# Hybrid SSD encoder with 16 experts: each expert's first weight chunk in transfers of 112, 8 and 8 partitions, and all finished rows normed ahead of the last sums

## The reference, cut to what matters

```python
def expert_choice_ffn(h, w_router, w_gate, w_up, w_down):
    ...
    cap = CAPACITY_FACTOR * n_tok // N_EXPERTS          # 64 and 32 tokens an expert
    probs = jax.nn.softmax(t.astype(jnp.float32) @ w_router.astype(jnp.float32), axis=-1)
    aff, idx = lax.top_k(probs.T, cap)
    xe = t[idx]
    hid = jax.nn.silu(jnp.einsum("ecd,edf->ecf", xe, w_gate)) * jnp.einsum("ecd,edf->ecf", xe, w_up)
    ye = jnp.einsum("ecf,efd->ecd", hid, w_down) * aff[..., None].astype(h.dtype)
    out = jnp.zeros_like(t).at[idx.reshape(-1)].add(ye.reshape(-1, d))
...
    x = x + expert_choice_ffn(rms_norm(x, norm_ffn_w), w_router, w_gate, w_up, w_down)
...
    return rms_norm(x, norm_final_w)
```

## Time and profile before

| | |
|---|---|
| median of 3 runs | 2410.2 us (2407.26 to 2411.43) |
| the profiled execution | 2407.7 us |
| its span | 2405.8 us |
| TensorE busy | 2370.5 us, 99% |
| VectorE, ScalarE, GpSimd busy | 1077.1, 519.3, 302.5 us |
| moved by DMA | 707.02 MB |
| chain that ended last | TensorE 47%, DMA 10% |

### The profile page before, as it was taken

One profiled execution on the slowest core, in us unless ns is written; L12 is line 12 of the kernel. 1 busy time (PEld: TensorE's weight loads), 2 busy tenths in 40 slices (PEclk: granted clock), 3 DMA queues, 4 the chain that ended last, 5 costly groups with the idle time before them and its releaser, 6 DMA issues.

```text
span 2405.8 us, 49544 instructions
## 1 busy us (share of the span) xinstructions
PE 2370.5 (99%) x21931; PEld 1625.6 (68%) x21931; DVE 1077.1 (45%) x2059; ACT 519.3 (22%) x1076; POOL 302.5 (13%) x417
## 2 busy tenths in 40 slices
PE   9999999999999999999999999999999999999997
PEld 8888999899898888745655455555555555444454
DVE  7989888888987634451221222122122112212213
ACT  6445444544534412200000000000000000000001
POOL 0422431341341000000000000000000000000001
PEclk9999999999999999999999999999999999999998
DMA  5233234223336545799999999999999999999996
GB/s 187 74 110 123 92 99 134 90 92 118 114 117 212 208 140 207 289 395 410 418 411 420 416 409 420 408 417 409 418 417 408 419 416 409 420 406 416 420 409 259
DMA packets 88646, 707.02 MB, mean 294 GB/s; under 512 B 11824, under 2 KB 16048, under 8 KB 51568
## 3 DMA queue, kind: packets, MB, share of 16 engines
q1 hardware_dynamic: 65504, 628.96, 64.4%
q0 software_dynamic: 14368, 56.80, 7.5%
q10 hardware_dynamic: 8560, 18.10, 2.0%
HBM read 669.76 MB, written 34.06 MB: 293 GB/s over the span
## 4 chain that ended last, share of the span: by engine, by line
PE 47%; DMA 10%; DVE 0%; issue 0%; POOL 0%; POOLq 0%; SPq 0%; ACT 0%; DVEq 0%
PE p_gu L2653 31%; PE p_y L2671 8%; DMA raw<-in_w_e 7%; PE p_y L2674 4%; PE p_z L2674 2%; DMA raw_first<-in_w_e 2%; DMA raw<-xa 1%; PE p_gu L1592 1%; DVE raw L2587 0%; DMA out<-raw 0%; DVE xg L2579 0%; POOLq L2725 0%; POOL out L2489 0%; PE off_banks L1606 0%; SPq L2421 0%
## 5 line engine op out<-in xcount | busy, mean ns | idle before, releaser
L2653 PE MATMUL p_gu<-raw,xT 128*32 128x512 f32 (+1 forms) x8160 | 888.6, 556 | 2.3 <-DMA raw<-in_w_e 2.2
L2653 PEld LDWEIGHTS p_gu<-raw,xT 128*32 128x32 f32 x8160 | 393.8, 110 | 362.8 <-issue 231.0
L2538 DVE SCALAR_TENSOR_TENSOR tg<-tg,p_gu 128x256 f32<-128x256 f32 (+1 forms) x144 | 57.4, 399 | 1051.6 <-ACT tg L2501 1047.1
L2671 PE MATMUL p_y<-raw,hidT 128*32 128x384 f32 x3744 | 433.3, 486 | 0.0
L1282 PE MATMUL pp<-h,wx_hi 128*128 128x256 f32 (+1 forms) x1664 | 423.9, 346 | 0.5 <-ACT fo L836 0.5
L2501 ACT ACTIVATE tg<-p_gu 128x256 f32<-128x256 f32 (+1 forms) x144 | 52.8, 367 | 1266.6 <-PE p_gu L2653 1249.0
L2674 PE MATMUL p_y<-raw,hidT 128*32 128x256 f32 x1248 | 319.5, 379 | 0.0
L1282 PEld LDWEIGHTS pp<-h,wx_hi 128*128 128x128 f32 x1664 | 282.9, 190 | 31.0 <-ACT fo L836 0.7
L1282 PE MATMUL pp<-h,wx_lo 128*128 128x256 f32 (+1 forms) x832 | 281.3, 338 | 0.0
L2674 PEld LDWEIGHTS p_y<-raw,hidT 128*32 128x32 f32 x1248 | 137.2, 110 | 100.1 <-issue 32.1
L2674 PE MATMUL p_z<-raw,hidT 128*32 128x256 f32 x624 | 184.8, 379 | 0.0
(11 more groups left out here) (297 smaller groups left out, 2951.1 us busy)
## 6 DMA issues: line engine op xcount, KB each, us to landing
raw<-in_w_e SPq DMA_DIRECT2D x185, 2048.0 KB, 32.0
raw<-in_w_e SPq DMA_DIRECT2D x58, 1536.0 KB, 32.5
raw_first<-in_w_e SPq DMA_DIRECT2D x23, 2048.0 KB, 33.3
w_raw<-in_w_x SPq DMA_DIRECT2D x48, 512.0 KB, 3.5
dec<-acs POOLq DMA_DIRECT2D x48, 512.0 KB, 4.8
raw<-in_w_e SPq DMA_DIRECT2D x16, 1024.0 KB, 32.6
w_raw<-in_w_g SPq DMA_DIRECT2D x24, 512.0 KB, 3.4
g_tab<-gx POOLq DMA_DIRECT2D x8, 1152.0 KB, 6.0
```

Source lines behind the costliest of these rows:

```text
L2538: dve.scalar_tensor_tensor(out=tg[:, r % 2, 0:w], in0=tg[:, r % 2, 0:w], scalar=1.0, in1=p[:, 0:w], op0=ALU.add, op1=ALU.mult).then_inc(s_ ...
L2653: mm = pe.matmul(p_gu[g][quad(q), 0:w], xT[:, e % 2, k * SLOTS + 32 * g:k * SLOTS + 32 * (g + 1)], slot[:, at:at + w], start=(k == 0), sto ...
L2671: pe.matmul(y_first[half][quad(g), :], hidden(g), w[:, half * 3 * P:(half + 1) * 3 * P], start=first, stop=last)
```

## The change

A chunk is loaded in pieces (`in_pieces`) if it is the first gate and up chunk of an expert and comes from the loop, which are 15 chunks. `load_part` then issues three transfers, of partitions 0 to 111, 112 to 119 and 120 to 127, each adding 16 to the slot's semaphore. `landings(c)` counts how much the semaphore of `c`'s slot has had with chunk `c`, and `loaded` waits for that. In the tail the roots are taken in groups of tiles 0 to 2, 3 and 4, and 5, and VectorE norms all six tiles ahead of `summed`. The squares stay behind the last tanh.

```diff
+PIECES = (slice(0, P - 16), slice(P - 16, P - 8), slice(P - 8, P))
+def in_pieces(c):
+    kind, b, i = chunk(c)
+    return c >= RAW and kind == "gu" and i == 0 and b % NB == 0
+def landings(c):
+    return sum(16 * (len(PIECES) if in_pieces(n) else 1) for n in range(c % RAW, c + 1, RAW))
...
-    sp.dma_start(raw[c % RAW][:, 0:w], src).then_inc(s_raw[c % RAW], 16)
+    for rows in PIECES if in_pieces(c) else (slice(0, P),):
+        sp.dma_start(raw[c % RAW][rows, 0:w], src[rows, :]).then_inc(s_raw[c % RAW], 16)
...
-        SQUARES_AT = ROUNDS - 1
-        NORMS_AT = ROUNDS - 1
-        ROOTS = (slice(0, 1), slice(1, 3), slice(3, NT))
-        FIRST_NORMS = 3
+        SQUARES_AT = {ROUNDS - 1: range(NT)}
+        ROOTS = (slice(0, NT // 2), slice(NT // 2, NT - 1), slice(NT - 1, NT))
...
-                if r == NORMS_AT:
-                    for t in range(FIRST_NORMS):
-                        norm(t)
+            for t in range(NT):
+                norm(t)
             summed(0)
             summed(1)
-            for t in range(FIRST_NORMS, NT):
-                norm(t)
...
-                pe.wait_ge(s_raw[c % RAW], (XT_LOADED if c % RAW < EARLY_RAW else 0) + 16 * (c // RAW + 1))
+                pe.wait_ge(s_raw[c % RAW], (XT_LOADED if c % RAW < EARLY_RAW else 0) + landings(c))
```

More of the change, by code:

```diff
@@ L2522, in _ @@
                         result(e)
-                if r == SQUARES_AT:
-                    for t in range(NT):
-                        square(t)
+                for t in SQUARES_AT.get(r, ()):
+                    square(t)
             act.wait_ge(f_row, 1)
```

## The result

The changed kernel takes 2634.16 us (median of 6 runs, 2630.86 to 2644.86), the kernel before 2408.55 (6 runs): 1.094 times the time, 95% interval 1.0919 to 1.096. The forecast was 2403.5 in a range up to 2422. 225 us were lost where 5 were expected to be gained.

What follows compares the result with a forecast made beforehand. Weight loads on the slowest DMA engines were taken to bound the last experts. Stall -4.79, squares -3.2 and new tail +2.7 gave -5.3 us; with half the median's excess given back, 2403.5 us, range 2399.5 to 2422.

Steps and rivals of the forecast that it cites:

- What bounds the kernel: In the last experts TensorE waits for weight chunks, 4.79 us in all, because the slowest DMA engines need 86.5 us an expert.
- The stall by growth and head start: TensorE's stall is lag growth, 1.34 us an expert, times 11.6 experts, less a prefetch head start of 10.7 us: 4.79 us.
- I take 0.63, since a row stays one packet of one engine: In the weight transfers, a 16 KB row of a narrow piece takes 0.63 us of its engine, as in whole loads.
- Rival 3: Narrow weight transfers are slow: 1.5 us an expert more on the nine-row engines, 2422 us in all; chance 0.13.
- Its bound from above: Row time in narrow weight transfers taken from the gather, 325 GB/s instead of 414: 1.27 times, applied to 9 rows.
- The estimate by the Trainium skill: 8 partitions reach two ports, so 128 KB takes 2.4 us instead of 0.63; a stall of 37 us, near 2446.
- Rival 1: The extra weight rows fall on the engines that lag: growth 1.97 us an expert, 10.1 us lost, 2420; chance 0.15.
- Were the eight the ones that do not lag: In the weight stream, the slowest engines would then lag 0.71 us an expert instead of 1.34: no stall, -4.79 us.
- That the instruction packets lie on the engines that lag: Eight engines lag together and carry all instruction packets seen; these cost 0.5 us an expert over sixteen engines, 1.0 over eight.
- The squares: In the tail, rows of xa land 4.6 us sooner against TensorE's end, so the squares follow the last tanh: -3.2 us.
- The new tail: Sums behind all six norms make the put wait for the last scaling: +2.7 us, or +1.8 with a short last root.
- The other roots end before VectorE wants them: In the tail, VectorE's norms never wait for roots after the first group; six norms run at 1.23 us each.

Runs made afterwards that it cites:

- the share alone: New tail, whole loads, plus four small transfers of 8 rows four partitions apart (0 to 31) behind each piece chunk, into unread columns: 2420.92 us, 8.8 over the new tail without them.
- one event at expert 2: New tail, pieces of 112, 8 and 8 partitions in expert 2 only, all other chunks whole: 2420.46 us; the same in expert 9 only: 2425.19 us.

## Why the prediction was wrong, point by point

**What bounds the kernel** held: TensorE waits for nothing but weights, and the slowest engines set the pace. The stall by growth and head start fits the run of the share alone, if the slowest engines are among its eight: a row more on these was to cost 7.4 us, and 8.8 were measured.

**The step that failed** is the price of the pieces: "I take 0.63, since a row stays one packet of one engine." A row does stay one packet, but its time depends on the other rows in flight with it. Measured, a row took some 1.15 us while the 112 rows passed and up to 2.3 while the 8-row pieces did, and on all sixteen engines. Three things were missed. The 112 rows were costed at nothing; an extra transfer of 112 partitions an expert costs 55 us by itself. The slow rate holds for the loads that run beside the pieces, not for nine rows of eight engines. And it holds from the first engine's arrival to the last one's departure, so engines that are out of step multiply it: 8.4 us for one event at expert 2, 13.1 at expert 9, and 222 / 15 = 14.8 each when every expert has one.

**Rival 3** named the mechanism and the side, and was off in size: 1.5 us an expert and 2422 against 14.8 and 2634. Its bound from above, 1.27 times a row's time from the gather, was no bound: the nearest row of the trace was of another kind of transfer, and it was applied to the wrong rows. The estimate by the Trainium skill, "SBUF — State Buffer", section "Door 1: The DMA port swizzle", 2446, had the better price for a piece of 8 rows (2.4 us, where rows took up to 2.3) and the same fault, that only eight engines pay.

**Number of engines.** That a short transfer takes eight engines was taken from a page alone. The packets now show it: 65744 - 65504 = 240 = 15 x 16, two times 8 completions for each chunk more, as the Trainium skill, "DMA: Bandwidth & Descriptors", section "Why a DMA increments its semaphore by 16 and not by 1", has it. That these are the lowest-numbered engines stands in that section too, and no row shows it.

**Rival 1** (the wrong eight) was priced at 7.4 us for the share and seems to be true in part, with two lagging engines among the eight. By the run of the share alone, the change would then have lost some 8.8 us even with free pieces, and not gained 4.8. So this step of the forecast, "Were the eight the ones that do not lag", most likely failed as well. In the changed kernel it is hidden: even shares cost as much. That the instruction packets lie on the engines that lag, as the prediction reads them, can't be told from the record, in which no packet names its engine; what the landings show is two groups of eight.

**Issues and completions** were costed at nothing, and cost nearly nothing: 2.6 us for thirty more transfers and 256-column rows.

**The squares** were to follow the last tanh at once (-3.2 us). They wait as before, 3.02 us. The engines ended later and not earlier, and TensorE with them; with whole loads the wait is 3.00.

**The new tail** was right in sum, and partly by luck. ScalarE, GpSimd and VectorE in the tail of the changed kernel:

```profile
2600.50 0.33 ACT L2514 ACTIVATE tg<-p_gu 128x192 f32<-128x192 f32 x1 [0.96 <-PE p_gu L2662]
2603.85 1.06 ACT L2529 ACTIVATE raw<-raw 128x1024 f32<-128x1024 f32 x1 [3.02 <-DMA raw<-xa]
```

```profile
2610.18 1.16 POOL L2489 TENSOR_SCALAR ssqf<-ssqf 128x2 f32<-128x2 f32 x1 [1.41 <-ACT raw L2529]
2611.42 1.62 POOL L2490 TENSOR_TENSOR rstdf<-ssqf,neg_half 128x2 f32<-128x2 f32 x1
...
2614.49 1.47 POOL L2490 TENSOR_TENSOR rstdf<-ssqf,neg_half 128x1 f32<-128x1 f32 x1
...
2621.22 0.55 POOL L2496 TENSOR_TENSOR rstdf<-ssqf,neg_half 96x1 f32<-96x1 f32 x1
2624.18 1.05 POOL L2502 DMA_INDIRECT out<-xg,idx_g  x1 [2.41 <-issue]
```

```profile
2608.80 3.68 DVE L2599 SCALAR_TENSOR_TENSOR raw<-raw,rstdf,nfin 128x1024 f32<-128x1024 f32 x3 [6.78 <-POOL rstdf L2490]
2613.07 2.48 DVE L2599 SCALAR_TENSOR_TENSOR raw<-raw,rstdf,nfin 128x1024 f32<-128x1024 f32 x2 [0.59 <-POOL rstdf L2490]
2615.99 1.28 DVE L2599 SCALAR_TENSOR_TENSOR raw<-raw,rstdf,nfin 128x1024 f32<-128x1024 f32 x1 [0.44 <-POOL rstdf L2490]
2617.19 0.61 DVE L2587 SCALAR_TENSOR_TENSOR xg<-p_y,aff,xg 96x384 f32<-96x384 f32 x1
...
2621.81 1.41 DVE L2637 SCALAR_TENSOR_TENSOR xg<-xg,rstdf,nfin 96x512 f32<-96x512 f32 x2 [1.86 <-POOL rstdf L2496]
```

From the first square to the put it takes 2624.18 - 2603.85 = 20.3 us, before 17.5: +2.8, where 2.7 was predicted. Two misses cancel. "The other roots end before VectorE wants them" was wrong: beside VectorE's norms the roots of two and of one column took 1.62 and 1.47 us, and the step ahead of the first of them 1.16. In the kernel before, with VectorE idle, two columns took 0.71 and that step 0.19. So the norms waited 0.59 + 0.44 = 1.0 us for them. The last root took 0.55, the short form, and not the 1.48 that I took: 0.9 less. The put is bound by the scaling, as predicted.

## What to carry to other kernels

Cut a load by columns, or take every second partition, if it has to be cut: here two transfers of 64 neighbouring partitions ran at about half rate, and 8-row ones took the loads beside them down as well. Price a new kind of transfer by what it does to the whole stream while it is in flight, not by the time of its own rows, and ask how long it is in flight when the engines are out of step. Where only the slowest engine counts, an average shift of work in the right direction is worth nothing if one slow engine gets more.

## What was not expected of the hardware, and what stays open

- Slow transfers slow the others: while pieces on eight engines passed, the sixteen moved 144 GB/s at full occupation, a third of the 414 of a whole stream; the kernel before moved 360 at that place.
- 64 neighbouring partitions moved 214 GB/s, 64 alternate ones 398, at the same place of the program. Whether the limit lies where the rows are written or where they are read in HBM, no run tells, since both changed together.
- The engines drift apart faster when pieces come in every expert, with equal halves too: from 3 us between first and last landing in expert 1 to 31 in expert 8, where whole loads end at 13.
- Why 112 neighbouring partitions are slow is open. By the table in the Trainium skill, "SBUF — State Buffer", section "Door 1: The DMA port swizzle", they reach all 16 ports, so that rule alone doesn't give it; which engine writes which row in such a transfer no row shows.
- Of the 225 us, 56 stand in the profile as TensorE's longer busy time. By the clock records of the traces TensorE ran at half speed (1.2 of 2.4 GHz) for some 121 us of the changed kernel and 21 of the kernel before; 100 us more at half speed would make up to 50 of the 56, by estimate. An example is 1910 to 1920 us, with a mean granted clock of 0.86, behind ten microseconds in which TensorE was busy for 6.4. How much of the 56 would be waiting at a full clock wasn't tried.
